# Two transformer blocks on one core: the seams between stages worked token tile by token tile

## The chip, the cores and the metric

The kernel runs on one core of a Trainium2 chip. The time is device microseconds (us) of one execution. Five engines work side by side, each through its own queue in order: PE (TensorE: LDWEIGHTS puts a stationary operand into the array, MATMUL streams a moving operand past it), DVE (VectorE), ACT (ScalarE), POOL (GpSimd), SP (SyncE), which here issues the DMAs. They meet through semaphores.

## What is computed

256 tokens of width 1024, float32. A first block (adaptive norm, three token mixers, output product, norm, a 16-expert mixture with top 2 of one group) ends in a norm; two layers of a second kind follow, and a final norm. The seams that this document is about lie between these steps:

```python
h = x                                        # the first block's output
for l in range(2):
    sh1, sc1, ga1, sh2, sc2, ga2, sh3, sc3, ga3 = split(silu(c) @ ada_w[l] + ada_b[l], 9)
    n = rms_norm(h, norm_g[l, 0]) * (1 + sc1) + sh1
    h = h + 0.5 * ga1 * swiglu(n, ffn_w_in[l, 0], ffn_w_out[l, 0])      # hidden width 2816
    n = rms_norm(h, norm_g[l, 1]) * (1 + sc2) + sh2
    h = h + ga2 * token_mixing(n, mix_w_in[l], ..., mix_w_out[l])       # q, k, v and gates first, mix_w_out last
    n = rms_norm(h, norm_g[l, 2]) * (1 + sc3) + sh3
    h = h + 0.5 * ga3 * swiglu(n, ffn_w_in[l, 1], ffn_w_out[l, 1])
return rms_norm(h, final_norm_g)
# swiglu: gate, up = split(n @ w_in); (silu(gate) * up) @ w_out.  rms_norm: x * rsqrt(mean(x*x) + eps) * g
```

A norm needs the whole row of a token, so it can't begin for a token before that token's last product is summed. It needs nothing of other tokens.

## The kernel before

**Weights.** All weights come as *units* of 128 x 2048 floats (1 MB) in one stream. SP loads a unit into one of three raw slots (`load`, L235 to L241). ACT rounds it to the first float32r half (`conv_hi`, L270) and DVE makes the rest, raw minus that (`conv_lo`, L276). The halves, too, have three slots (`RING = 3`), so `conv_hi` of unit c waits until PE has used unit c-3. Every product is done three times (`mm3`, L343 to L345: high x high, and the two mixed ones) to keep float32 accuracy.

**Which operand is stationary.** In `project` (q, k, v and gates of the mixer; 48 matmuls a unit) the normed tokens are stationary, 128 at a time, and 256 weight columns move; it works tile by tile already. In `rows_product` (down and output products; 24 matmuls a unit) 128 tokens are stationary and 512 weight columns move. In `pe_gate_up` (gate and up products of a feed-forward; 48 matmuls a unit) a 128 x 128 block of the *weights* is stationary, and all 256 tokens move: 2 blocks of columns x 8 depths x 3 products. The hidden layer comes out turned that way, ready for the down product.

**A feed-forward** has 11 groups of 256 hidden columns: gate unit, up unit, and the down unit of the group before. `hidden_order` lays the stream out in that order. ACT takes the silu, DVE multiplies, both split the result. DVE also makes the modulation vectors of later layers from `ada` weights (`half_step`, L304 and L310; two 1 MB loads each from the same SP queue), PE sums them (L324), DVE adds the bias (L338), and PE waits for that before it uses the bank again. `last_down` does the last unit one tile after the other.

**The seam.** After the last product of a stage, all in this order: DVE multiplies tile 0's sum by the gate row and adds it to x (`residual`, L493, L496), then tile 1's. ACT squares tile 0 (L386), POOL makes the root (L395, L397), ACT scales tile 0 (L390) and squares tile 1, POOL makes its root, DVE scales it (L402). PE turns both tiles (`norm_pe`, L418, 8 transposes each) into four banks that hold both tiles side by side, ACT and DVE scale, shift and split them (`spread_act`, `spread_dve`), PE broadcasts the gate (`gate_pe`, L482, 16 matmuls) and ACT copies it out. Then the next stage's first unit begins. There are six such seams (first block's output product to the router; feed-forward to mixer and output product to feed-forward in each layer; feed-forward to feed-forward between the layers), one behind the mixture of experts with two norms in a row, and the final norm.

**Order and loops.** Each engine's order is written out by hand. Groups of a feed-forward, and the 12 q, k and v units, run in hardware loops (`Fori`).

Of the kernel before, what the change touches and what calls it, by code (L numbers as in the profile page):

```python
# [26 lines left out]
P = 128  # L27
# [60 lines left out]
EARLY_HALVES = 20  # L88
FFN_HALVES = {(0, 0): (20, 10), (0, 1): (30, 10), (1, 0): (40, 8), (1, 1): (48, 0)}
# [32 lines left out]
def bass_network(nc, W, AD, x_in, ctx_in, s1_in, s2_in, k1_in, masks_in, gf_in, out):  # L122
    with ExitStack() as ctx:
# [50 lines left out]
        ntmp = z(0, 1024).rearrange("p (b n) -> p b n", b=2)  # L174
# [108 lines left out]
        def load_half(sp, v, e=0):  # L283

            for i in range(2):
                if v > PE_HALVES:
                    sp.wait_ge(ada_used, e * 4 + (2 * (v - 1 - PE_HALVES) + i + 1))
                elif v > 0:
                    sp.wait_ge(ada_used_pe, 2 * (v - 1) + i + 1)
                src = AD[2 * v + i] if isinstance(e, int) and e == 0 else AD[bass.ds(e * 4 + (2 * v + i), 1)].rearrange(  # L290
                    "o p n -> p (o n)")
                sp.dma_start(ada[:, i], src).then_inc(ada_landed[i], 16)

        def half_step(dve, v, n, e=0):

            vv, i, k = v - PE_HALVES, n // 4, n % 4
            cond = 0 if v < B1_HALVES else 16
            if k == 0:
                dve.wait_ge(ada_landed[i], e * 32 + 16 * (v + 1))
            w, c, a = ada[:, i, 512 * k:512 * k + 512], cs[:, cond + n:cond + n + 1], acc[:, v % 2]  # L300
            if n == 0:
                if vv >= 2:
                    dve.wait_ge(ada_sum.sem, e * 2 + (vv - 1))
                ins = nc.vector.tensor_scalar(a, w, c, None, ALU.mult)  # L304
            else:
                if n == 4:
                    dve.wait_ge(ada_used, e * 4 + (2 * vv + 1))
                else:
                    dve.wait_ge(acc_step, e * 12 + (6 * vv + (n if n < 4 else n - 1)))
# [3 lines left out]
        def half_steps(dve, v, i, e=0):  # L313
            for n in range(4 * i, 4 * i + 4):
                half_step(dve, v, n, e)

        def half_sum(pe, v, bank, e=0):

            vv = v - PE_HALVES
            pe.wait_ge(ada_used, e * 4 + (2 * vv + 2))  # L320
            if vv >= 2:
                pe.wait_ge(ada_out.sem, e * 2 + (vv - 1))
# [5 lines left out]
        def half_out(dve, v, bank, e=0):  # L328

            dve.wait_ge(ada_sum.sem, e * 2 + (v - PE_HALVES + 1))  # L330
            b0 = S1["bada"].start
            if isinstance(e, int) and e == 0:
                dst = mod1[:, 4 * v:4 * v + 4] if v < B1_HALVES else mod2[:, 4 * (v - B1_HALVES):4 * (v - B1_HALVES) + 4]
                bias = s1[:, b0 + 4 * v:b0 + 4 * v + 4]
            else:
                dst = mod2[:, bass.ds(e * 8 + 4 * (v - B1_HALVES), 4)]
                bias = s1[:, bass.ds(e * 8 + (b0 + 4 * v), 4)]
            nc.vector.tensor_tensor(dst, PS[:, bank, 0:4], bias, ALU.add).then_inc(*ada_out.up)  # L338
# [8 lines left out]
        def project(u, xh, xl, bank, tiles=range(NT), lo_at=None):  # L347

            wh, wl = (w.rearrange("p (k n) -> p k n", k=DC) for w in u)
            for t in tiles:  # L350
                for k in range(DC):
                    if lo_at and t == 0 and k % 2 == 0:
                        nc.tensor.wait_ge(*lo_at[k // 2])
# [14 lines left out]
        NB = (0, 1, 4, 5)  # L368

        class Norm:  # L370
            def __init__(self, name, per, stats_only=False):
# [4 lines left out]
                self.xa, self.xd, self.am, self.full = (sig(f"{name}_{n}", per) for n in ("scaled0", "scaled1", "factors", "full"))  # L376
# [4 lines left out]
        def norm_act(act, N, k, l, src, dst, x_at=(None, None)):  # L381

            for t in range(NT):
                if x_at[t]:
                    act.wait_ge(*x_at[t])
                nc.scalar.activation(dst[:, t], src[:, t], ACT.Square, scale=D ** -0.5,  # L386
                                     accum_out=st[:, t:t + 1]).then_inc(*N.ss.up)
                if t == 0:
                    act.wait_ge(*N.rstd.at(2 * k, l))
                    nc.scalar.activation(dst[:, 0], src[:, 0], ACT.Copy, scale=st[:, 4:5]).then_inc(*N.xa.up)  # L390
# [8 lines left out]

        def norm_dve(dve, N, k, l, src, dst):  # L400
            dve.wait_ge(*N.rstd.at(2 * k + 1, l))
            nc.vector.tensor_scalar(dst[:, 1], src[:, 1], st[:, 5:6], None, ALU.mult).then_inc(*N.xd.up)  # L402
# [10 lines left out]
        def norm_pe(pe, N, k, l, src, banks):  # L413
            for t, scaled in enumerate((N.xa, N.xd)):
                pe.wait_ge(*scaled.at(k, l))
                for c in range(DC):
                    o = (c % 2) * 256 + t * P
                    ins = nc.tensor.transpose(PS[:, banks[c // 2], o:o + P], src[:, t, c * P:(c + 1) * P], ident)  # L418
                    if t and c % 2:
                        ins.then_inc(*N.turned.up)  # L420

        def spread_act(act, N, k, l, hi, shift, banks, am_):

            act.wait_ge(*N.am.at(k, l))
            for b in range(4):
                act.wait_ge(*N.turned.at(4 * k + b, l))
                for c in range(2):
                    ins = nc.scalar.activation(hi[:, 2 * b + c], PS[:, banks[b], c * 256:(c + 1) * 256], ACT.Identity,
                                               scale=am_[:, 2 * b + c:2 * b + c + 1], bias=shift[:, 2 * b + c:2 * b + c + 1])
                ins.then_inc(*N.hi.up)  # L430
            act.wait_ge(*N.lo.at(4 * k + 1, l))
            for c in range(2):
                ins = nc.scalar.activation(ntmp[:, 1, c * 256:(c + 1) * 256], PS[:, banks[3], c * 256:(c + 1) * 256],
                                           ACT.Identity, scale=am_[:, 6 + c:7 + c], bias=shift[:, 6 + c:7 + c])
            ins.then_inc(*N.full.up)
# [4 lines left out]
        def spread_dve(dve, N, k, l, hi, lo, shift, banks, am_):  # L440
            dve.drain()
            for b in range(4):
                dve.wait_ge(*N.hi.at(4 * k + b, l))
                if b < 3:
                    for c in range(2):
                        nc.vector.tensor_scalar(ntmp[:, b % 2, c * 256:(c + 1) * 256], PS[:, banks[b], c * 256:(c + 1) * 256],
                                                am_[:, 2 * b + c:2 * b + c + 1], shift[:, 2 * b + c:2 * b + c + 1],
                                                ALU.mult, ALU.add)
                    dve.drain()
                else:  # L450
                    dve.wait_ge(*N.full.at(k, l))
# [45 lines left out]

        def at_gate(c0, g):
            return c0 + (3 * g - 1 if g else 0)
# [1808 lines left out]
```

## Time and profile before

| | us |
|---|---|
| median of 3 runs | 2260.92 (2258.34 to 2265.45) |
| profiled execution, its own time | 2261.06 |
| its span, first to last instruction | 2259.3 |
| PE busy | 2008.0 |
| DVE busy | 1388.1 |
| ACT busy | 998.5 |
| mean granted PE clock | 0.924 of 2.4 GHz |

Times of rows count from the span's start. "Busy" of PE is the union of its instructions' durations, which overlap when matmuls follow one another; how far apart they start is read from start times, or from how many (x) lie in a window. PEclk 1.00 is 2.4 GHz, 0.50 is 1.2 GHz.

### The profile page before, as it was taken

The numbers are of one execution on the slowest core, as the hardware profiler recorded it, in microseconds if no ns is written. First come the engines' busy times: TensorE is split into PE (matmuls) and PEld (weight loads), VectorE is DVE, ScalarE is ACT, GpSimd is POOL, SyncE is SP. The second block draws the span as 40 slices with busy tenths as digits, with TensorE's granted clock in tenths as the row PEclk, the third lists the DMA queues.
The fourth block names the chain that finished last, engine by engine and source line by source line (L and its number), as shares of the span: only waits on it lengthen the run. The fifth ranks groups of instructions, "written<-read, shape, count | busy, mean of one in ns | idle before, by whom it ended". The sixth has DMA issues, their size and how long they took to land.

```text
span 2259.3 us, 31283 instructions
## 1 busy us (share of the span) xinstructions
PE 2008.0 (89%) x12630; PEld 1769.3 (78%) x12630; DVE 1388.1 (61%) x1440; ACT 998.5 (44%) x1149; POOL 91.7 (4%) x103
## 2 busy tenths in 40 slices
PE   6878977999999699988797799989998979968997
PEld 1855667888888699978776689978997967857997
DVE  0875755899998677754433677766765343355445
ACT  2423324777777433344345343343334433444333
POOL 0230010000000100010000000000001000000000
PEclk9876786999999899989898899999999989989999
DMA  7563452899998287634312457755763532223553
GB/s 271 199 231 111 164 207 76 324 370 358 348 352 337 114 322 297 254 124 174 106 63 75 149 220 282 283 218 208 299 238 131 176 109 108 75 77 133 191 183 150
DMA packets 63845, 457.93 MB, mean 203 GB/s; under 512 B 7040, under 2 KB 7296, under 8 KB 8832
## 3 DMA queue, kind: packets, MB, share of 16 engines
q1 hardware_dynamic: 63744, 456.51, 53.4%
q8 instruction: 72, 1.18, 0.2%
q14 instruction: 29, 0.24, 0.0%
HBM read 455.43 MB, written 1.05 MB: 202 GB/s over the span
## 4 chain that ended last, share of the span: by engine, by line
issue 40%; PE 39%; DVE 10%; ACT 5%; DMA 3%; POOL 1%; DVEq 1%; POOLq 1%; SPq 0%; ACTq 0%
PE PS L343 10%; PE PS L344 10%; PE PS L345 10%; DVE wlo L276 3%; ACT whi L270 3%; DVE acc L310 2%; DMA ada<-in_ada 2%; PE PS L1158 1%; PE PS L324 1%; DMA raw<-in_stream 1%; PE PS L1701 1%; PE PS L1109 1%; PE PS L1174 1%; POOLq L396 1%; POOL st L397 1%
## 5 line engine op out<-in xcount | busy, mean ns | idle before, releaser
L276 DVE TENSOR_TENSOR wlo<-raw,whi 128x2048 fp32r<-128x2048 f32 x285 | 653.7, 2295 | 514.3 <-ACT whi L270 514.3
L270 ACT ACTIVATE whi<-raw 128x2048 fp32r<-128x2048 f32 x285 | 545.0, 1913 | 496.9 <-PE PS L345 461.1
L343 PE MATMUL PS<-whi,hhi 128*128 128x256 f32 (+1 forms) x1360 | 450.6, 331 | 18.1 <-DVE hlo L466 8.6
L344 PE MATMUL PS<-wlo,hhi 128*128 128x256 f32 (+1 forms) x1360 | 441.4, 325 | 0.0
L345 PE MATMUL PS<-whi,hlo 128*128 128x256 f32 (+1 forms) x1360 | 441.3, 324 | 0.0
L343 PE MATMUL PS<-hhi,whi 128*128 128x256 f32 x1408 | 402.2, 286 | 10.3 <-DVE mod L338 7.7
L344 PE MATMUL PS<-hlo,whi 128*128 128x256 f32 x1408 | 400.2, 284 | 0.0
L345 PE MATMUL PS<-hhi,wlo 128*128 128x256 f32 x1408 | 400.1, 284 | 0.0
L343 PEld LDWEIGHTS PS<-whi,hhi 128*128 128x128 f32 x1360 | 266.5, 196 | 41.1 <-DVE hlo L466 10.1
L343 PEld LDWEIGHTS PS<-hhi,whi 128*128 128x128 f32 x1408 | 272.0, 193 | 14.2 <-DVE wlo L276 8.9
L345 PEld LDWEIGHTS PS<-whi,hlo 128*128 128x128 f32 x1360 | 265.6, 195 | 19.2
L344 PEld LDWEIGHTS PS<-wlo,hhi 128*128 128x128 f32 x1360 | 266.5, 196 | 17.7
L344 PEld LDWEIGHTS PS<-hlo,whi 128*128 128x128 f32 x1408 | 272.1, 193 | 1.4
L345 PEld LDWEIGHTS PS<-hhi,wlo 128*128 128x128 f32 x1408 | 272.0, 193 | 0.0
L343 PE MATMUL PS<-whi,zr 128*128 128x512 f32 (+2 forms) x624 | 233.0, 376 | 21.0 <-DVE zr L1936 11.1
L310 DVE SCALAR_TENSOR_TENSOR acc<-ada,cs,acc 128x512 f32<-128x512 f32 x308 | 238.6, 775 | 10.8 <-DMA ada<-in_ada 1.4
L345 PE MATMUL PS<-whi,zr 128*128 128x512 f32 (+2 forms) x624 | 228.4, 369 | 0.0
L344 PE MATMUL PS<-wlo,zr 128*128 128x512 f32 (+2 forms) x624 | 228.2, 369 | 0.0
L343 PEld LDWEIGHTS PS<-whi,zr 128*128 128x128 f32 (+1 forms) x624 | 114.8, 184 | 41.7 <-DVE zr L1936 11.2
L345 PEld LDWEIGHTS PS<-whi,zr 128*128 128x128 f32 (+1 forms) x624 | 114.7, 184 | 20.8
L344 PEld LDWEIGHTS PS<-wlo,zr 128*128 128x128 f32 (+1 forms) x624 | 114.9, 184 | 18.8
L276 DVE TENSOR_TENSOR wlo<-ada,whi 128x2048 fp32r<-128x2048 f32 x48 | 109.9, 2292 | 12.7 <-ACT whi L270 12.5
(349 smaller groups left out, 1895.5 us busy)
## 6 DMA issues: line engine op xcount, KB each, us to landing
raw<-in_stream SPq DMA_DIRECT2D x285, 1024.0 KB, 4.8
ada<-in_ada SPq DMA_DIRECT2D x96, 1024.0 KB, 4.8
ada<-in_stream SPq DMA_DIRECT2D x48, 1024.0 KB, 4.9
xs<-in_x SPq DMA_DIRECT2D x1, 1024.0 KB, 7.7
Z<-in_ctx SPq DMA_DIRECT2D x1, 1024.0 KB, 9.8
masks<-in_masks SPq DMA_DIRECT2D x2, 512.0 KB, 6.8
Z<-in_gfinal SPq DMA_DIRECT2D x2, 512.0 KB, 7.4
y_out<-Z SPq DMA_DIRECT2D x2, 512.0 KB, 2.6
```

The source lines that it names most:

```text
L270: nc.scalar.activation(whi[:, s], src, ACT.Copy).then_inc(hi_ready, 1)
L276: nc.vector.tensor_tensor(wlo[:, s], src, whi[:, s].bitcast(F32), ALU.subtract).then_inc(lo_ready, 1)
L310: ins = nc.vector.scalar_tensor_tensor(a, w, c, a, ALU.mult, ALU.add)
L324: ins = nc.tensor.matmul(PS[:, bank, c:c + 1], acc[:, v % 2, c * P:(c + 1) * P], ones[:, 0:1], start=True, stop=True)
L343: nc.tensor.matmul(out_, ah, bh, start=start, stop=False, skip_group_check=check)
L344: nc.tensor.matmul(out_, ah, bl, start=False, stop=False, skip_group_check=check)
L345: return nc.tensor.matmul(out_, al, bh, start=False, stop=stop, skip_group_check=check)
L396: pool.drain()
L397: nc.gpsimd.tensor_tensor(st[:, 4 + t:5 + t], st[:, 2 + t:3 + t], k1[:, K1["half"]][:, 0:1], ALU.pow).then_inc(*N.rstd.up)
L1109: ins = nc.tensor.matmul(PS[0:2, 6 + v % 2, :], cs[:, n:16:8], ada[:, i, 512 * k:512 * k + 512], start=n == 0, stop=n == 7)
L1158: nc.tensor.matmul(PS[:, i % 2], q, k, start=i >= 16, stop=True).then_inc(*s_mm.up)
L1174: ins = nc.tensor.matmul(PS[:, 4 + (p // 8) % 2, 64 * (p % 8):64 * (p % 8) + 64], pt[:, p % 2, c * P:(c + 1) * P], v[c], start=c == 0, sto ...
```

## The change

`pe_gate_up` becomes `gate_up_part` with a tile, and the head of a feed-forward does gate 0, up 0 and gate 1 for tile 0, then for tile 1:

```diff
+        def gate_up_part(pe, g, j, c0, E0, tile=None, lo_at=None):
+            wh, wl = (w.rearrange("p (k n) -> p k n", k=DC) for w in unit(pe, at_gate(c0, g) + j, E0))
+            tok = slice(0, S) if tile is None else slice(tile * P, tile * P + P)
+            for f in range(2):
+                for k in range(DC):
+                    w = slice(f * P, (f + 1) * P)
+                    if lo_at and f == 0 and k % 4 == 0:
+                        pe.wait_ge(*lo_at[2 * tile + k // 4])
+                    ins = mm3(PS[:, 2 * (g % 2) + f, j * 256 + tok.start:j * 256 + tok.stop], wh[:, k, w], wl[:, k, w],
+                              hhi[:, k, tok], hlo[:, k, tok], k == 0, k == DC - 1)
+            if tile != 0:
+                ins.then_inc(unit_used, 1)
...
+            head = ((0, 0), (0, 1), (1, 0))
+            for i, (g, j) in enumerate(head):
+                gate_up_part(pe, g, j, c0, E0, 0, None if i else lo_at(k, l))
+                if i == 1:
+                    norm_pe(pe, N2, k, l, 1, xn, TB)
+            for i, (g, j) in enumerate(head):
+                gate_up_part(pe, g, j, c0, E0, 1, None if i else lo_at(k, l))
+            gate_pe(pe, N2, k, l, 6)
```

The down units of the last three groups move to the end of the stream and are done for tile 0, then for tile 1, with the next stage's first transposes between the second and the third:

```diff
+        def last_downs(pe, c0, E0, h0, between):
             for t in range(NT):
+                for g in range(TAIL, FFN_GROUPS):
+                    pe.wait_ge(hlo_done, h0 + (g + 1))
+                    u = unit(pe, at_down(c0, g), E0)
+                    for kk in range(2):
+                        ins = rows_product(u, kk, hid_hi[:, hid(g), kk], hid_lo[:, hid(g), kk], 4, False, False, True, (t,))
+                    if t:
+                        ins.then_inc(unit_used, 1)
+                    if t and g == FFN_GROUPS - 2:
+                        between()
                 for b in range(4 + 2 * t, 6 + 2 * t):
```

`out_product` does its first unit for both tiles, the other three by tile, with `between` in the same place. The mixer does its first three units for tile 0 (tile 1's transposes before the third), then for tile 1. The seam's other engines:

```diff
+        def norm_act(act, N, k, l, shift, c, e, x_at):
+            square_act(act, N, k, l, 0, xs, xn, x_at[0])
+            conv_hi(act, c, e)
+            spread_act(act, N, k, l, 0, hhi, shift, TB, am)
+            conv_hi(act, c + 1, e)
+            conv_hi(act, c + 2, e)
+            square_act(act, N, k, l, 1, xs, xn, x_at[1])
+            scale_act(act, N, k, l, xs, xn)
+            spread_act(act, N, k, l, 1, hhi, shift, TB, am)
+
+        def norm_dve(dve, N, k, l, shift, c, e, y_at):
+            residual(dve, N.x_new, 0, y_at[0])
+            scale_dve(dve, N, k, l, xs, xn)
+            conv_lo(dve, c, e)
+            spread_dve(dve, N, k, l, 0, hhi, hlo, shift, TB, am)
+            residual(dve, N.x_new, 1, y_at[1])
+            conv_lo(dve, c + 1, e)
+            dve.wait_ge(*N.rstd.at(2 * k + 1, l))
+            conv_lo(dve, c + 2, e)
+            spread_dve(dve, N, k, l, 1, hhi, hlo, shift, TB, am)
```

`scale_dve` scales tile 0 and `scale_act` tile 1, the other way round than before. `spread_act` and `spread_dve` now work on one tile: ACT writes the first four blocks of 128 columns into a buffer, DVE the other four, ACT copies each half out rounded, DVE subtracts. The gate's diagonal on POOL waits for tile 1's last split (`N2.lo`), its broadcast on PE comes after the three first units. In the last two groups of a feed-forward, which have no down product beside them, the conversions stand behind silu and behind the rounding:

```diff
+                if g <= TAIL:
+                    conv_hi(act, c + RING, E0)
+                act_silu(act, g, c0, E0, h0)
+                if g > TAIL:
+                    conv_hi(act, at_gate(c0, g) + RING, E0)
+                else:
+                    conv_hi(act, c + 1 + RING, E0)
+                act_hi(act, g, c0, E0, h0)
```

Behind the mixture of experts, two conversions that stood ahead of the norm stand behind its two tiles' steps. The conversions behind the last feed-forward are gone. All `Fori` loops are written out.

## Rows read from the trace of the kernel before

**Rows 1.** of the page: busy time, and the chain that ended last, by engine.
```profile
PE 2008.0 (89%) x12630; PEld 1769.3 (78%) x12630; DVE 1388.1 (61%) x1440; ACT 998.5 (44%) x1149; POOL 91.7 (4%) x103
...
issue 40%; PE 39%; DVE 10%; ACT 5%; DMA 3%; POOL 1%; DVEq 1%; POOLq 1%; SPq 0%; ACTq 0%
```

**Rows 2.** waits of PE, whole span: us in total, times, longest us.
```profile
PE PS L418 <- ACT xn L390: 51.3, 7, 13.4
...
PE PS L343 <- DVE mod L338: 7.7, 3, 3.2
```

**Rows 3.** windows around five stage boundaries: us, busy (xcount) by engine, PEclk, DMA, GB/s.
```profile
745.40:787.00 41.60, 25.09 (x181) 23.95 (x181) 28.44 (x31) 16.77 (x25) 10.56 (x9) 0.79 0.20 76
957.00:1002.50 45.50, 36.94 (x229) 33.50 (x230) 26.52 (x25) 19.81 (x24) 7.81 (x10) 0.85 0.31 111
1267.10:1322.40 55.30, 47.16 (x276) 41.98 (x277) 30.36 (x31) 22.70 (x25) 4.40 (x5) 0.91 0.38 144
1494.20:1541.20 47.00, 37.20 (x235) 33.21 (x235) 30.50 (x33) 19.89 (x24) 5.22 (x5) 0.89 0.39 153
1713.00:1759.20 46.20, 36.52 (x231) 32.46 (x230) 27.13 (x24) 20.46 (x25) 7.27 (x10) 0.89 0.31 113
```

**Rows 4.** windows of PE alone: us, PE busy (xcount), PEclk, DMA share, GB/s.
```profile
1317.00:1328.00 11.00, 11.00 (x94) 1.00 0.46 167
1275.00:1285.00 10.00, 10.00 (x46) 1.00 0.43 133
1102.00:1104.00 2.00, 2.00 (x37) 1.00 0.03 8
351.00:354.00 3.00, 3.00 (x16) 0.50 0.06 11
395.00:741.00 346.00, 346.00 (x1630) 1.00 0.90 349
1131.00:1165.00 34.00, 32.42 (x226) 0.98 0.18 63
183.00:245.00 62.00, 57.23 (x188) 0.50 0.32 117
```

**Rows 5.** timeline of PE, matmuls with 256 columns after a boundary.
```profile
984.99 0.41 PE L344 MATMUL PS<-wlo,hhi 128*128 128x256 f32 x1
985.20 0.41 PE L345 MATMUL PS<-whi,hlo 128*128 128x256 f32 x1
```

**Rows 6.** window of the same stretch, all engines, for its PEclk.
```profile
984.70:985.50 0.80, 0.80 (x6) 0.80 (x5) 0.80 (x3) 0.59 (x2) 0.00 (x0) 0.50 0.00 0
```

**Rows 7.** timeline, group 9 of the first feed-forward: start us, us, engine, line, count.
```profile
938.14 0.98 PEld L324 LDWEIGHTS PS<-k,acc 128*128 128x128 f32 x8
938.26 0.95 PE L324 MATMUL PS<-k,acc 128*128 128x1 f32 x8
...
938.95 1.91 ACT L270 ACTIVATE whi<-raw 128x2048 fp32r<-128x2048 f32 x1
...
940.89 2.29 DVE L276 TENSOR_TENSOR wlo<-raw,whi 128x2048 fp32r<-128x2048 f32 x1 [0.54 <-ACT whi L270]
```

**Rows 8.** timeline at the boundary after the first output product: the norm chain.
```profile
1288.31 1.22 DVE L493 TENSOR_TENSOR Z<-PS,row 128x1024 f32<-128x1024 f32 x1
...
1291.50 1.06 ACT L386 ACTIVATE xn<-xs 128x1024 f32<-128x1024 f32 x1 [5.76 <-DVE xs L496]
...
1292.72 1.23 POOL L395 TENSOR_TENSOR st<-st,k 128x1 f32<-128x1 f32 x1 [2.34 <-ACT xn L386]
...
1295.86 1.97 PE L418 MATMUL PS<-k,xn 128*128 128x128 f32 x8 [6.70 <-ACT xn L390]
...
1297.84 0.75 DVE L402 TENSOR_SCALAR xn<-xs,st 128x1024 f32<-128x1024 f32 x1 [3.94 <-POOL st L397]
...
1299.43 3.76 ACT L428 ACTIVATE hhi<-PS,mod,am 128x256 fp32r<-128x256 f32 x8 [0.78 <-PE PS L418]
...
1301.56 0.69 DVE L452 TENSOR_TENSOR hlo<-Z,hhi 128x512 fp32r<-128x512 f32 x1
```

More of the change, by code:

```diff
@@ L326, in half_sum, with half_out @@
             ins.then_inc(*ada_sum.up)
[L328 to L338, printed above, removed]
+        def half_out(dve, v, bank):
+            dve.wait_ge(*ada_sum.at(v - PE_HALVES))
+            b0 = S1["bada"].start + 4 * v
+            dst = mod1[:, 4 * v:4 * v + 4] if v < B1_HALVES else mod2[:, 4 * (v - B1_HALVES):4 * (v - B1_HALVES) + 4]
+            nc.vector.tensor_tensor(dst, PS[:, bank, 0:4], s1[:, b0:b0 + 4], ALU.add).then_inc(*ada_out.up)
         def mm3(out_, ah, al, bh, bl, start, stop, check=False):
@@ L375, in __init__ @@
                     return
-                self.xa, self.xd, self.am, self.full = (sig(f"{name}_{n}", per) for n in ("scaled0", "scaled1", "factors", "full"))
+                self.scaled = [sig(f"{name}_scaled{t}", per) for t in range(NT)]
+                self.fullB = sig(f"{name}_full", 2 * per)
+                self.am = sig(f"{name}_factors", per)
                 self.turned, self.hi, self.lo = (sig(f"{name}_{n}", 4 * per) for n in ("turned", "hi", "lo"))
@@ L411, in turn @@
                     ins.then_inc(*done.up)
[L413 to L422, printed above, removed]
-            act.wait_ge(*N.am.at(k, l))
[L425 to L435, printed above, removed]
@@ L487, in gate_act @@
             nc.scalar.activation(row[:, :], PS[:, bank:bank + 2].rearrange("p b n -> p (b n)"), ACT.Copy).then_inc(*N.row.up)
-        def residual(dve, done, y_at, banks=((4, 5), (6, 7)), tmp=ytmp):
-            for t in range(NT):
-                dve.wait_ge(*y_at[t])
-                nc.vector.tensor_tensor(tmp[:, t], PS[:, banks[t][0]:banks[t][1] + 1].rearrange("p b n -> p (b n)"), row[:, :],
-                                        ALU.mult)
-                dve.drain()
-                nc.vector.tensor_tensor(xs[:, t], xs[:, t], tmp[:, t], ALU.add).then_inc(*done.up)
@@ new lines, in hidden_pe @@
+        def hidden_pe(pe, c0, E0, h0, halves, k, l, between):
+            v0, nh = halves
+            head = ((0, 0), (0, 1), (1, 0))
[6 more added lines that the diff above has]
+            gate_pe(pe, N2, k, l, 6)
+            for g in range(1, FFN_GROUPS):
+                steps, sums = g < nh, g <= nh
+                if sums and g > 1:
+                    pe.wait_ge(*ada_out.at(v0 + g - 2 - PE_HALVES))
+                elif nh and g > 1:
+                    pe.wait_ge(*ada_out.at(v0 + nh - 1 - PE_HALVES))
+                for j in range(int(g == 1), 2):
+                    gate_up_part(pe, g, j, c0, E0)
+                if sums:
+                    pe.wait_ge(h_made, h0 + g)
+                    half_sum(pe, v0 + g - 1, 2 * (1 - g % 2))
+                if g == 1:
+                    pe.wait_ge(*N2.row.at(k, l))
+                    clear_sums(pe)
+                if g <= TAIL:
+                    pe_down(pe, g - 1, c0, E0, h0)
+            last_downs(pe, c0, E0, h0, between)
@@ L2121, in _ @@
                 hidden_sp(sp, FF0, E0, FFN_HALVES[l, 0])
-                with sp.Fori(0, MIX_UNITS // RING) as e:
-                    for j in range(RING):
-                        load(sp, QK0 + RING + j, E0 + e)
+                for j in range(MIX_UNITS):
+                    load(sp, QK0 + RING + j, E0)
                 hidden_sp(sp, FF1, E0, FFN_HALVES[l, 1])
@@ L2219, in hidden_order @@
     seq = [gate[0], up[0]]
-    for g in range(1, n):
+    for g in range(1, n - 2):
         seq += [gate[g], up[g], down[g - 1]]
-    return seq + [down[n - 1]]
+    for g in range(n - 2, n):
+        seq += [gate[g], up[g]]
+    return seq + down[n - 3:]
 def halves(w):
```

522 lines of the change are left out of this document (260 added, 262 removed).

## The prediction

> **What bounds the kernel now.** I began with the page. PE is busy for 2008 of 2259 us and holds the largest named share of the chain that ended last [rows 1], so time goes if PE work goes, or PE's waits. The waits view names the largest wait: transposes for the scaled tile, 51.3 us in 7 pieces, the longest 13.4 [rows 2]. Those are the seams. The window view then prices a seam with all around it: what PE does, and at what clock [rows 3]. In the five windows PE's clock averages 0.79 to 0.91; the reader is to see that a seam costs twice, in waiting and in matmuls at 1.2 GHz behind it. Between seams PE has no gap: 346 us of 346 in the mixture of experts [rows 4]. Last I read how far apart matmuls of each shape start, since the change makes new shapes.
>
> **The distance of matmuls.** In a window with x of them it is its length over x, less the two or three under way at its start. At full clock: 256 moving columns 0.120 us (94 in 11 us), 512 columns 0.227 (46 in 10), 128 columns past a stationary of only 32 columns 0.060 (37 in 2) [rows 4]. At half clock, 20 moving columns past a stationary of 128: 16 in 3 us, 0.213 [rows 4]; and 256 moving columns: 985.20 - 984.99, also 0.21 [rows 5], at clock 0.50 [rows 6]. So with a full stationary operand 20 columns cost as much as 256: the loading sets the distance. At full clock, eight loads with one moving column take 0.98 us [rows 7], 0.12 each with the last one's run-out in it, so a little less from start to start; and half of 0.213, the clock being twice as fast, is 0.107. Hence a load of 128 columns costs about 0.112, hidden behind 256 moving columns but not behind 128.
>
> This is where the change pays. In `project`, `rows_product` and the output product the tokens are stationary, so doing a unit by tile adds nothing: the same matmuls in another order. In a feed-forward's head the weights are stationary: 3 units x 48 = 144 matmuls of 256 columns become 288 of 128, each with its load. At 0.112 they take 32.3 us in place of 144 x 0.120 = 17.3: +15.0 us in each of four feed-forwards, 60 in all. The bounds: not below the 0.060 of the small stationary (17.3 us, adds nothing), not above the 0.120 of 256 columns (34.6 us, +17.3, 69 in all). I take 0.112, as only the 0.060 row has another stationary, and it is the smaller load that makes it fast.
>
> The Trainium skill (TensorE: Matmul & The Clock Gate, LDWEIGHTS (loading the stationary operand)) gives a load as its columns over 1.2 GHz, 107 ns for 128: the trace agrees within 6 ns. The same page, in Back-to-back issue gap, gives a stream of load and matmul pairs at 128 columns about 81 ns each; by that the term would be some 6 us each and 24 in all. No row here shows a full load under 0.11. I keep it as a rival.
>
> **Seam by seam.** PE work first, then waits. Work common to all: 16 transposes and 16 gate matmuls at 0.112, 2.0 (with their turnaround) and 1.8.
>
> *The norm chain of a tile.* Before: multiply begins 1288.31, ACT's square 1291.50, POOL 1292.72, transposes 1295.86 [rows 8]. That is 7.5 us. Now DVE scales tile 0 (0.75, where ACT's stands for 1.1), and POOL's diagonal no longer runs beside the add, which I put at 0.6: some 6.6. Beside it PE has tile 1 of two units, 24 x 0.227 = 5.4. So the transposes come 1.25 late. From them to the first split block I reckon four small scalings (under ACT's 3.76 / 8 = 0.47 each), a copy of about 0.6 and a subtraction of 0.69 [rows 8], 3.3; PE has the third unit's tile 1, 2.7: late by 0.2 to 0.6.
>
> *Feed-forward to mixer, twice.* Work: three down units 72 x 0.227 = 16.3, closing sums 0.9, 2.0, three units 17.3, gate 1.8: 38.3. Waits: the second down unit can only be converted behind the last silu. Silu done 0.8 after the last up unit, ACT 1.9, DVE 2.3 [rows 7]: 5.0, against 2.7 of the first down unit's tile 0. That wait is new, 2.3 us (1.3 in layer 0, where the L324 sums of 0.95 lie in it), and 0.2 for the third. Transposes 1.25, split 0.2. The mixer's second unit then waits for DVE, which must finish the split of tile 0, tile 1's residual (2.5) and the conversion (2.3): 2.55 late. Sum of waits 5.5 and 6.5, so 43.9 and 44.8. Before, the same span without one down unit (5.45) was 45.5 and 46.2 [rows 3], so 51.0 and 51.6: -7.1 and -6.8.
>
> *Output product to feed-forward, twice.* Work: 96 x 0.227 = 21.8, 2.0, 32.3, 1.8, clearing 0.9: 58.8. Waits 1.25 and 0.6. Here the longer tile-0 part (16 us) covers all of tile 1's chain. 60.6 against 55.3 [rows 3]; the second layer's seam repeats it: +5.3 each.
>
> *Feed-forward to feed-forward.* 16.3 + 0.9 + 2.0 + 32.3 + 1.8 + 0.9 = 54.2, waits 1.3, 0.2, 1.25, 0.6: 57.6. Before 47.0 [rows 3] + 5.45 = 52.4: +5.2.
>
> *Behind the mixture of experts.* Nothing of the old stage is left to lie beside the norms. Two conversions leave the way of the final norm (4.6 of DVE), but one still stands between the tiles; I reckon the first matmul 4 us earlier, at 18.4 of the window. Then 288 x 0.112, 2.4 for a start at half clock, 1.0 + 1.8 + 0.9: 56.8 against 41.6 [rows 3]: +15.2.
>
> *The rest.* Start of the first block, seam to the router (all 256 tokens are needed, so only a part overlaps) and the final norm: each has something earlier and something later (the last gains the two conversions on DVE and pays the 2.3 us wait). Together +0.6, bounds -6 and +8 by one chain of rows 8 gained or lost.
>
> *A wait that goes.* PE waits 7.7 us in three pieces for the modulation's bias (L338) early in three feed-forwards [rows 2]: after a seam SP's queue holds the next unit's load behind two `ada` loads that wait for DVE. The longer head gives that queue time for what it has to bring. I take it as gone, and with it the half clock behind the two longer ones, which I put at 4.5 us (an estimate: windows with such waits stand at 0.84 to 0.89 in rows 3): -12.2. Bounds: 0 and -12.2.
>
> *Half clock at the new seams.* The waits left are shorter than the old ones, but come one behind the other. Every old seam had some half clock [rows 3]. For the two mixer seams I take 1.7 each, 3.4; bounds 0 and 8.
>
> *Written-out loops.* Instructions come from memory as before. 346 us of written-out code show PE without a gap [rows 4]: 0. [...]
>
> **Sum**, on the span of 2259.3: 15.2 + 5.3 + 5.3 + 5.2 - 7.1 - 6.8 + 0.6 - 12.2 + 3.4 = +8.9, so 2268.2; with the 1.8 between span and time 2270.0. The profiled execution (2261.06) is within 0.2 of the median (2260.92), so the same number stands for the median.
>
> **Rivals.**
> *A. Loads hidden behind 128 columns* (each pair 0.060 to 0.081). For: at 0.060 the array can take a pair that fast [rows 4]. Against: rows 4, 5 and 7, three cases with a full load. At 0.060 the head is 15.0 us shorter in each feed-forward, but tile 1's chain is then only covered by half: some 4 of it come back each time. 2270 - 60 + 16 = 2226. This is the faster case. By the skill's 81 ns it would be 2270 - 36 = 2234.
> *B. The heads run at half clock.* In 62 us of attention PE was busy for 57 and the clock stayed at 0.50; with 20 columns per load it stayed there too [rows 4]. At 128 columns per load the array streams half of the time. For it: those rows. Against it: 34 us of small matmuls in the mixer at 0.98 [rows 4]. It decides when the clock doesn't rise again behind a seam: each head takes up to 288 x (0.213 - 0.112) = 29 us more. In one to four of the heads: 2299 to 2386.
> *C. The chains are wholly covered* and nothing of my waits appears: 5.5 + 6.5 + 1.9 x 2 + 3.4 + 3.4 = 22 less, 2248. For: they rest on orders of queues that I worked out. Against: the silu's place ahead of the conversion is in the code.
> *D. The wait for the bias stays*: 2282.
>
> **Chances.** Forecast 0.58 (2270, own range 2256 to 2282), A 0.10, B 0.14, C 0.10, D 0.08. A measurement of this kernel tells 0.3%, 6.8 us, from no change. Faster by more: A, C and a little of the forecast: 0.20. Slower by more: B, D and about two thirds of the forecast: 0.60. Within: 0.20. The range leaves out A and half of B: 2246 to 2305.
>
> **What would show it.** In the changed trace, gate and up matmuls of 128 columns: their distance at full clock, 0.112 (right) or near 0.06 (A), and PEclk over the heads (B). A gap of 2.3 us ahead of the second-to-last down unit's tile 0, and one of 2.5 ahead of the mixer's second unit. Waits for the scaled tile down from 51 to some 15. No wait for L338 early in a feed-forward. The forecast fails if PE's busy time doesn't grow by some 50 us.

## The result and the profile after

| | before | after |
|---|---|---|
| median, us | 2259.63 (4 runs, 2256.13 to 2265.45) | 2287.93 (4 runs, 2284.42 to 2288.71) |
| profiled execution, its own time | 2261.06 | 2284.42 |
| its span | 2259.3 | 2282.7 |
| PE busy | 2008.0 | 2062.2 |
| mean granted PE clock | 0.924 | 0.932 |

Ratio 1.0113, 95% interval 1.009 to 1.0136: slower. 2270 was forecast, with a range of 2246 to 2305. The sign and the main term were right; the sum was +8.9 where the spans differ by 23.4 us (the medians by 28.3). The result lies in the wide range, which had room for the rivals, but outside the forecast's own 2256 to 2282.

Busy time of the changed kernel, the page's row (its answer to the first row of [rows 1]):

```profile
PE 2062.2 (90%) x13206; PEld 1823.3 (80%) x13206; DVE 1369.9 (60%) x1455; ACT 996.3 (44%) x1164; POOL 83.2 (4%) x103
```

PE has 576 more matmuls (4 heads x 144) and is 54 us busier, while DVE has 18 us less. The waits view of PE (engine, line, releaser: us in all, times, longest) answers to [rows 2]:

```profile
PE PS L427 <- DVE xn L404: 13.2, 1, 13.2
...
PE PS L351 <- DVE mod L346: 12.4, 5, 4.7
PE PS L351 <- DVE wlo L277: 11.3, 6, 2.2
```

L427 is the old L418, L351 the old L343, L346 the old L338, L277 the old L276. Of the 51.3 us for the scaled tile, 13.2 are left in this row, and 7.9 more for ACT's half at the router. The wait for the bias has grown from 7.7 to 12.4, with a longest of 4.7, where I had struck it out. The six waits for the weights' conversion are the ones that I forecast: four at the ends of the feed-forwards, two at the mixer's second unit.

The five boundaries again, same columns as [rows 3], each from the matching instruction. Three of the five hold one down unit (5.45 us) that the old windows don't: the second, fourth and fifth.

```profile
741.50:805.30 63.80, 48.07 (x319) 47.70 (x320) 26.45 (x33) 19.41 (x27) 9.21 (x9) 0.70 0.14 50
977.10:1020.30 43.20, 39.42 (x255) 34.38 (x254) 28.05 (x29) 24.68 (x30) 6.72 (x10) 1.00 0.38 131
1282.90:1341.70 58.80, 58.00 (x417) 53.55 (x417) 30.19 (x34) 22.24 (x26) 3.86 (x5) 1.00 0.36 134
1512.70:1568.10 55.40, 53.82 (x398) 49.04 (x398) 33.70 (x38) 23.15 (x27) 3.85 (x5) 1.00 0.41 153
1730.30:1777.10 46.80, 42.08 (x253) 36.91 (x252) 27.91 (x28) 25.15 (x30) 6.72 (x10) 0.93 0.35 123
```

In the last four PE now has 0.8 to 4.7 us of gaps where it had 8 to 10, at clock 0.93 to 1.00 where it had 0.85 to 0.91: the tiles do cover each other's norm chains. But the third is 3.5 us longer than before all the same, because it is full of loads (288 matmuls of 128 columns in place of 144 of 256). And in the first, behind the mixture of experts, the clock fell from 0.79 to 0.70, and it is 22 us longer.

How far apart the new matmuls start, from windows of PE alone (us, PE busy (xcount), PEclk, DMA share, GB/s), inside the heads:

```profile
1318.00:1328.00 10.00, 10.00 (x93) 1.00 0.15 60
...
785.00:795.00 10.00, 10.00 (x92) 1.00 0.00 0
...
762.00:772.00 10.00, 10.00 (x48) 0.50 0.00 0
```

92 or 93 matmuls of 128 columns in 10 us, less the two or three under way: 0.110 to 0.111 us each. At half clock it is 0.213. So the load of 128 stationary columns sets the distance, and rival A is out. The head behind the mixture of experts ran tile 0's first 96 matmuls, all that stand ahead of tile 1's transposes, at 0.213.

The timeline around 957 us (start, us, engine, line, count; the bracket is the idle time before and its releaser) shows the wait that I had not foreseen:

```profile
957.04 0.95 PE L337 MATMUL PS<-k,acc 128*128 128x1 f32 x8
957.24 0.60 ACT L560 ACTIVATE Z<-PS 128x512 f32<-128x512 f32 x1 [9.54 <-PE PS L353]
957.73 1.90 ACT L271 ACTIVATE whi<-raw 128x2048 fp32r<-128x2048 f32 x1
957.86 0.69 DVE L572 TENSOR_TENSOR Z<-Z,PS 128x512 f32<-128x512 f32 x1 [5.08 <-ACT Z L560]
959.53 0.62 ACT L567 ACTIVATE zr<-Z 128x512 fp32r<-128x512 f32 x1
959.66 2.29 DVE L277 TENSOR_TENSOR wlo<-raw,whi 128x2048 fp32r<-128x2048 f32 x1 [1.11 <-ACT whi L271]
960.05 1.90 ACT L271 ACTIVATE whi<-raw 128x2048 fp32r<-128x2048 f32 x1
961.87 0.68 DVE L576 TENSOR_TENSOR zr<-Z,zr 128x512 fp32r<-128x512 f32 x1
...
962.47 0.15 DVE L346 TENSOR_TENSOR mod<-PS,s 128x4 f32<-128x4 f32 x1
...
962.68 0.58 PE L351 MATMUL PS<-hhi,whi 128*128 128x256 f32 x1 [4.70 <-DVE mod L346]
```

PE sums the modulation (L337) and wants that bank again for its next gate unit. DVE frees it by adding the bias, 0.15 us of work, but does so last: behind a conversion, which itself waits for ACT, and behind the hidden layer's split. Before, a down product of 5.45 us stood between PE's two steps and covered this. The same add in the kernel before, 5.45 us behind PE's sums at 938.26, and PE's next gate unit, which doesn't wait:

```profile
943.71 0.15 DVE L338 TENSOR_TENSOR mod<-PS,s 128x4 f32<-128x4 f32 x1
...
944.64 0.28 PE L343 MATMUL PS<-hhi,whi 128*128 128x256 f32 x1
```

The change took the down products of the last three groups away, and with them the cover. It happens in both feed-forwards of layer 0, at 958 and at 1493 us, 4.70 us each time, and each leaves half clock behind:

```profile
1496.40:1503.20 6.80, 5.22 (x24) 0.50 0.46 154
960.50:967.30 6.80, 4.62 (x21) 0.50 0.47 154
```

### The profile page after: what moved, and what is told of

It is laid out like the page before. It is cut to its first block, busy times and chain, and to the rows that moved or that the text cites. A ratio compares the mean times of both kernels' runs of the same rounds, so it can differ in the third digit from the quotient of the medians.

```text
span 2282.7 us, 30949 instructions
## 1 busy us (share of the span) xinstructions
PE 2062.2 (90%) x13206; PEld 1823.3 (80%) x13206; DVE 1369.9 (60%) x1455; ACT 996.3 (44%) x1164; POOL 83.2 (4%) x103
## 4 chain that ended last, share of the span: by engine, by line
issue 80%; PE 8%; DVE 5%; ACT 2%; DMA 2%; POOL 1%; DVEq 0%; POOLq 0%; ACTq 0%; SPq 0%
DVE acc L324 2%; DMA ada<-in_ada 2%; DVE wlo L277 1%; PE PS L351 1%; PE PS L353 1%; PE PS L352 1%; PE PS L1182 1%; PE PS L1131 1%; ACT whi L271 1%; PE PS L1198 1%; POOL Z L483 1%; DVE hlo L460 1%; PE PS L1189 1%; ACT Z L439 1%; PE PS L337 0%
## 5 line engine op out<-in xcount | busy, mean ns | idle before, releaser
L277 DVE TENSOR_TENSOR wlo<-raw,whi 128x2048 fp32r<-128x2048 f32 x282 | 646.9, 2295 | 467.5 <-ACT whi L271 461.8
L271 ACT ACTIVATE whi<-raw 128x2048 fp32r<-128x2048 f32 x282 | 538.3, 1912 | 410.6 <-PE PS L353 379.8
L351 PE MATMUL PS<-hhi,whi 128*128 128x256 f32 (+1 forms) x1600 | 457.5, 286 | 16.5 <-DVE mod L346 12.4
L351 PE MATMUL PS<-whi,hhi 128*128 128x256 f32 (+1 forms) x1360 | 451.0, 332 | 22.4 <-DVE hlo L473 8.9
L352 PE MATMUL PS<-hlo,whi 128*128 128x256 f32 (+1 forms) x1600 | 456.4, 285 | 0.0
L353 PE MATMUL PS<-hhi,wlo 128*128 128x256 f32 (+1 forms) x1600 | 456.2, 285 | 0.0
L351 PEld LDWEIGHTS PS<-hhi,whi 128*128 128x128 f32 x1600 | 314.0, 196 | 20.7 <-DVE mod L346 13.8
L352 PEld LDWEIGHTS PS<-hlo,whi 128*128 128x128 f32 x1600 | 314.0, 196 | 1.1
L353 PEld LDWEIGHTS PS<-hhi,wlo 128*128 128x128 f32 x1600 | 313.9, 196 | 0.0
L351 PEld LDWEIGHTS PS<-whi,hhi 128*128 128x128 f32 x1360 | 266.8, 196 | 46.3 <-DVE hlo L473 10.4
L351 PE MATMUL PS<-whi,zr 128*128 128x512 f32 (+2 forms) x624 | 234.2, 378 | 28.3 <-DVE zr L1976 11.1
L351 PEld LDWEIGHTS PS<-whi,zr 128*128 128x128 f32 (+1 forms) x624 | 115.2, 185 | 50.3 <-issue 19.7
L560 ACT ACTIVATE Z<-PS 128x512 f32<-128x512 f32 x44 | 26.3, 597 | 209.7 <-PE PS L353 209.7
```

What stands on the lines that cost most here:

```text
L271: nc.scalar.activation(whi[:, s], src, ACT.Copy).then_inc(hi_ready, 1)
L277: nc.vector.tensor_tensor(wlo[:, s], src, whi[:, s].bitcast(F32), ALU.subtract).then_inc(lo_ready, 1)
L351: nc.tensor.matmul(out_, ah, bh, start=start, stop=False, skip_group_check=check)
L352: nc.tensor.matmul(out_, ah, bl, start=False, stop=False, skip_group_check=check)
L353: return nc.tensor.matmul(out_, al, bh, start=False, stop=stop, skip_group_check=check)
L560: nc.scalar.activation(hs, PS[:, p:p + 2, 0:256], ACT.Silu).then_inc(silu_done, 1)
```

## The experiments

Ratios are to the kernel before, timed in the same session, with 95% intervals. The changed kernel itself stands at 1.0113. Of the edits, lines that only select a form, and the wait of a whole head for both tiles' splits, are left out.

**heads_whole.** The heads' matmuls have 256 columns again; everything else is as changed.

```diff
-            for i, (g, j) in enumerate(head):
-                gate_up_part(pe, g, j, c0, E0, 0, None if i else lo_at(k, l))
-                if i == 1:
-                    norm_pe(pe, N2, k, l, 1, xn, TB)
-            for i, (g, j) in enumerate(head):
-                gate_up_part(pe, g, j, c0, E0, 1, None if i else lo_at(k, l))
+            norm_pe(pe, N2, k, l, 1, xn, TB)
+            for i, (g, j) in enumerate(head):
+                gate_up_part(pe, g, j, c0, E0, None, None if i else lo_at(k, l))
```

> The changed kernel with the four feed-forward heads not split: tile 1 is turned first, then gate 0, up 0 and gate 1 run with 256 moving tokens. Everything else of the change stays. Theory (loading 128 columns sets the distance, 0.111 us in the changed trace, 0.213 at half clock): the heads' 288 matmuls become 144 at 0.120, 15 us less of PE work in each of four, and about 10 us more in the head behind the mixture of experts, which ran at half clock; given back is the wait for tile 1's chain, about 11 us in three heads and a few us in the first. From the traces: 4.6 us less in each of three, 18 to 22 less in the first, 32 to 36 us less in all than the changed kernel's 2288: about 2254. Rival (the split itself is free and the loss lies elsewhere, in new waits at the ends of the feed-forwards): PE work is the same and the chain is exposed, so 25 to 35 us slower than the changed kernel, about 2318.

Measured: 0.9954 (0.9939 to 0.997), 2253.5 us. Undoing this one part wins back 1.6% and leaves a kernel faster than the one before, so the split heads are what turned the change's sign. The waits view now shows what they had covered, PE waiting for tile 1 (one of the four, 7.9 us at the router, is in the changed kernel too):

```profile
PE PS L427 <- ACT xn L400: 31.3, 4, 7.9
```

From the start of tile 0's transposes to the gate broadcast, the first head takes 26.5 us in place of 48.9; the three others 35.1, 35.6 and 35.1 in place of 37.6. So without the split each of those wins 2.0 to 2.5 us, not the 4.6 expected, and the first makes up most of the gain (22.3 us).

**head_one_whole.** The same edit at the first head alone, `if (k, l) == (0, 0)`.

> As the changed kernel, but only the head behind the mixture of experts is not split (nothing of an old stage lies beside its norms). Theory (that head pays the loads, 15 us, and on top half clock, since 128 columns to a load don't bring the clock up, some 10 us): 18 to 22 us less than 2288, about 2268, and PEclk rises to 1.00 within a few us of the head's start where it stayed at 0.50 for 24 us. Rival (the clock there is only the time of day after a 13 us wait, whatever runs): the clock stays at 0.50 for the same 24 us, and at 0.213 for 256 columns too the whole head takes 31 us at most, so 5 to 10 us less.

Measured: 0.9985 (0.9974 to 0.9997), 2259.3 us; the profiled span is 26.8 us shorter than the changed kernel's. That is 80% of what all four whole heads bring, and more than the 18 to 22 expected. 22.3 us of it lie in the head. Another 3.0 are half clock at the second mixer seam, which the changed kernel's trace has and this one hasn't, though the edit touches nothing there; the rest is spread over later stages. The same windows of PE as above, now from this kernel: the stretch ahead of the head and its start, then 10 us inside it.

```profile
746.00:766.00 20.00, 7.08 (x32) 0.50 0.31 105
766.50:776.50 10.00, 10.00 (x86) 1.00 0.01 2
```

PE's first gate matmul is at 762.6 here, at half clock, and the full clock is back at 766.5, 4 us later. In the changed kernel it began at 759.2 and the clock stayed at 0.50 until 783.0, 24 us with no gap. Ahead of it stand 16 transposes and a gap of 3.9 us here, 8 transposes and a gap of 2.5 us there, and it starts 3.4 us later; otherwise only the columns per load differ. (86 in 10 us, less those under way, is again 0.120.)

**warm_up.** The changed kernel, with dummy matmuls ahead of the first head, where PE idles:

```diff
+                for i in range(56):
+                    nc.tensor.matmul(PS[:, 4], zb[:, 0:P], zb[:, :], start=True, stop=True)
                 norm_pe(pe, N2, 0, 0, 0, xn, TB)
+                for i in range(11):
+                    nc.tensor.matmul(PS[:, 4], zb[:, 0:P], zb[:, :], start=True, stop=True)
```

> The changed kernel, with 56 dummy matmuls of 512 bf16 columns ahead of the first head's first transposes (PE was idle there) and 11 behind them; nothing else. In the changed kernel the head behind the mixture of experts began at clock 0.50 and its 96 matmuls of tile 0 took 20.7 us, 0.213 each, without a gap. Theory: 128 columns per load don't bring the clock up, but don't let it fall either; begun at full clock, tile 0's part takes 96 x 0.111 = 10.7 us, so 10 to 12 us less than the changed kernel, about 1.005 times the kernel before. Rival: in this stretch the clock is down for another reason (the rest of the chip, or the columns per load alone), and the head falls back to 0.50 however it begins: no gain, about 1.011.

Measured: 1.0046 (1.0032 to 1.0059), 2274.8 us, 0.7% or some 15 us under the changed kernel (10.0 by the spans; 11.4 from tile 0's transposes to the gate broadcast). Windows of PE: the dummies, tile 0's 96 matmuls, tile 1's and the rest of tile 0's 192.

```profile
742.00:754.20 12.20, 12.13 (x54) 0.98 0.20 75
759.50:770.30 10.80, 10.80 (x97) 1.00 0.01 2
771.10:792.60 21.50, 21.50 (x195) 1.00 0.11 38
```

Begun at full clock, the same split head stays there for all of its 33 us, and tile 0's part takes 10.9 us instead of 20.7. The rival (it falls back whatever comes before) is out.

**bias_early.** In the last two groups DVE adds the bias right behind the hidden product:

```diff
                 dve_h(dve, g, h0)
+                if sums and g > TAIL:
+                    half_out(dve, v0 + g - 1, 2 * (1 - g % 2))
...
-                if sums:
+                if sums and g <= TAIL:
                     half_out(dve, v0 + g - 1, 2 * (1 - g % 2))
```

> The changed kernel with one order changed: in the last two groups of a feed-forward DVE adds the modulation bias (L346) right behind the hidden product, ahead of the weight conversion. Theory: PE's two waits of 4.70 us ahead of the last gate unit in the two feed-forwards with modulation work there come from this order, since the down unit that used to cover them has moved to the end; they shrink to about 0.9, and the half clock behind them (2.2 us each) goes: 10 to 12 us less than 2288, about 2277. Rival (they wait for the conversion of the last gate unit's weights as well): same time, the wait now named after L277.

Measured: 1.0044 (1.003 to 1.0057), 2271.4 us; the span is 13.7 us shorter than the changed kernel's. The wait is down from 4.70 to 0.69, and no half clock follows; of this kernel's timeline:

```profile
959.70 0.69 DVE L572 TENSOR_TENSOR Z<-Z,PS 128x512 f32<-128x512 f32 x1 [5.08 <-ACT Z L560]
960.31 0.15 DVE L346 TENSOR_TENSOR mod<-PS,s 128x4 f32<-128x4 f32 x1
960.52 0.39 PE L351 MATMUL PS<-hhi,whi 128*128 128x256 f32 x1 [0.69 <-DVE mod L346]
```

2 x (4.70 - 0.69) is 8.0 us of waiting. From the gate broadcast to the next stage's first transposes the two feed-forwards of layer 0 are 4.2 and 6.4 us shorter, 10.6 in all, with the clock behind the waits. The other 3.0 us are again the half clock at the second mixer seam, where this edit changes no wait. So the trace shows some 11 us for moving one instruction of 0.15 us.

**conv_early.** In the last two groups the conversion of the next unit stands ahead of silu (on ACT) and of the half steps (on DVE), as in the other groups:

```diff
-                if g <= TAIL:
-                    conv_hi(act, c + RING, E0)
+                conv_hi(act, at_gate(c0, g) + RING, E0)
                 act_silu(act, g, c0, E0, h0)
-                if g > TAIL:
-                    conv_hi(act, at_gate(c0, g) + RING, E0)
-                else:
+                if g <= TAIL:
                     conv_hi(act, c + 1 + RING, E0)
...
```

> The changed kernel with the conversion of the last two groups' next unit put back ahead of silu on ACT and ahead of the hidden product on DVE. Theory: the waits of 1.25, 1.25, 2.16 and 2.16 us between the first and second down unit's tile 0 go, with one stretch of half clock behind: 7 to 9 us less than 2288, about 2280. The two 4.70 us waits get a little shorter too, as DVE converts unit 29 before the hidden product instead of behind it: up to 4 more. Rival (the second down unit then waits for its load or its slot instead): no change.

Measured: 1.0066 (1.004 to 1.0091), 2275.5 us. The waits of PE in this kernel, against 12.4 (longest 4.7) and 11.3 in the changed one:

```profile
PE PS L351 <- DVE mod L346: 8.5, 5, 2.7
...
PE PS L351 <- DVE wlo L277: 6.1, 4, 2.2
```

The forecast wait for the second down unit was real, and the conversion's place in the queue made it: it is gone in layer 0 (1.25 us, twice) and down from 2.16 to 0.83, twice, in layer 1. The bias wait shrinks too, since a conversion no longer stands ahead of it.

**loops_written_out.** The kernel before, `with X.Fori(a, b) as e:` replaced by `for e in range(a, b):` in all six places.

> The kernel before with all six of its hardware loops written out, nothing else. My prediction put this part of the change at 0: ratio 0.998 to 1.002. [...] One more row speaks for a small gain: from the first block's seam to the router the changed kernel was 4 us ahead of the kernel before.

Measured: 0.9992 (0.9979 to 1.0004). No effect of this part is seen either way; and the changed kernel's 4 us lead at the router isn't from it.

**heads_whole_early.** heads_whole, bias_early and conv_early together (edits as above).

> The changed kernel with three edits together: the heads of the feed-forwards whole (256 columns), the bias added right behind the hidden product in the last groups, and the conversions of the last groups ahead of silu. Heads whole alone stood at 0.9954, bias early and conversions early took 0.7% and 0.5% off the changed kernel. If these are separate losses, the sum is 0.9954 - 0.006 - 0.002 (the two share the 4.7 us waits): 0.986 to 0.990, about 2235 us. Rival: with the heads whole the waits in the last groups are already covered otherwise: 0.995.

Measured: 0.9894 (0.9872 to 0.9915), 2240.7 us. The losses are separate but for the overlap that was reckoned with; the result is at the upper end of what was expected.

**one_unit_by_tile.** On top of that, the first unit of the three later heads by tile:

```diff
-                norm_pe(pe, N2, k, l, 1, xn, TB)
-                for i, (g, j) in enumerate(head):
-                    gate_up_part(pe, g, j, c0, E0, None, None if i else lo_at(k, l))
+                gate_up_part(pe, 0, 0, c0, E0, 0, lo_at(k, l))
+                norm_pe(pe, N2, k, l, 1, xn, TB)
+                gate_up_part(pe, 0, 0, c0, E0, 1, lo_at(k, l))
+                for i, (g, j) in enumerate(head[1:]):
+                    gate_up_part(pe, g, j, c0, E0)
```

> The same combined kernel, but in the three later heads the first unit (48 matmuls of 256 columns) is done tile by tile, 96 of 128. Cost by my prices: 96 x 0.111 - 48 x 0.120 = 4.9 us a head. Gain: with whole heads PE waits 7.9, 7.5 and 7.9 us for tile 1's transposes, with some 13.6 us at half clock behind; tile 0's part (5.3 us) covers 5.3 of it. Theory: gain and cost cancel, within 0.2% of the combined kernel, with the shorter half clock as a small gain (up to 2 us a head). Rival: doing work by tile with stationary weights never pays: 3 x 4.9 = 15 us, 0.65%, slower.

Measured: 0.9944 (0.9927 to 0.9961), 2250.7 us: 10 us slower than the combined kernel, so I was wrong and the rival nearer. Windows of PE at the head after the first output product: tile 0's 48 matmuls, tile 1's 48, and the first of 256 columns behind them.

```profile
1279.70:1285.20 5.50, 5.50 (x48) 1.00 1.01 427
1290.70:1301.10 10.40, 10.37 (x49) 0.50 0.15 61
1301.10:1305.10 4.00, 4.00 (x20) 0.50 0.00 0
```

Between tile 0's and tile 1's part PE waited 1.7 and 2.7 us, the clock fell, and tile 1's part took twice its time at 0.213 each. Again the clock rose only 4 us after the first matmul of 256 columns.

**whole_kept_warm and one_unit_kept_warm.** Both kernels with dummy matmuls in the waits of the heads. The first:

```diff
+                for i in range(0 if (k, l) == (0, 0) else 34):
+                    nc.tensor.matmul(PS[:, 4], zb[:, 0:P], zb[:, :], start=True, stop=True)
                 norm_pe(pe, N2, k, l, 1, xn, TB)
+                for i in range(15 if (k, l) == (0, 0) else 9):
+                    nc.tensor.matmul(PS[:, 6], zb[:, 0:P], zb[:, :], start=True, stop=True)
```

and 56 ahead of the first head's transposes, as in warm_up.

> The combined kernel (heads whole, bias and conversions early) with dummy matmuls in PE's waits at the four heads: 56 and 15 around the first head's transposes, 34 and 9 around tile 1's transposes at the other three, each 512 bf16 columns into a bank that is free there; they took 0.227 each in the run before. The combined kernel has some 14 us at clock 0.50 at each of the three heads, in which PE does 16 transposes or part of them and some 4 us of matmuls, and 20 at the first. Kept at full clock these save about 2.5 us at each of the three and 3.2 at the first: 10 us, ratio 0.985 against 0.9894. Rival: the dummies themselves delay the head, or the chip takes the clock away later instead: 0.989 to 0.993.

> The kernel with one unit of the three later heads by tile, with dummy matmuls in its waits (7 ahead of tile 1's transposes, 11 behind them; 56 and 15 at the first head). Without them it stood at 0.9944, 10 us above the combined kernel where I had expected none, and in its trace tile 1's 48 matmuls of 128 columns took 10.2 us, at clock 0.50, which lasted 17 us instead of 14. Theory: that half clock is the whole excess, 3 x 5 us; with the clock kept, cost (4.9) and cover (5.3) cancel: 0.984 to 0.987, the same as the combined kernel kept warm. Rival: the split costs more by itself: 5 us or more (0.2%) above that kernel.

Measured: 0.9835 (0.9822 to 0.9848), 2226.7 us, the fastest of all; and 0.985 (0.9834 to 0.9867), 2230.1 us. One window of PE from the second kernel, tile 1's part, for the 10.4 us above:

```profile
1289.30:1294.80 5.50, 5.47 (x49) 1.00 0.27 113
```

With the clock kept, the two kernels are 3.4 us apart instead of 10, and their intervals overlap. From tile 0's transposes to the gate broadcast, this head takes 32.9 us whole and 32.6 with one unit split, and the two later ones the same; without the dummies it was 35.0 and 39.2. So the split cancels out, as reckoned, and its loss was the clock. The fill itself brought 0.6%, 14 us where I expected 10. (A dummy starts 0.216 us behind the one before, not 0.227.) The kernel before was not run with dummies, so how much of the 0.9835 the fill would bring without any work by tile isn't shown.

**heads_by_tile_mended.** The changed kernel with its heads as they were, and warm_up, bias_early and conv_early together.

> The changed kernel with its heads by tile as they were (three units, 128 columns per load), and all else mended: warm start of the first head, bias and conversions early in the last groups. It says what the heads by tile cost at their best, against the whole heads kept warm (0.9835). Theory: 4 x 15 us of loads less the waits for tile 1 that they cover at the three later heads (7.9 + 2.3, 7.5 + 2.3, 7.9 + 2.3 = 30) and some 4 at the first: 60 - 34 = 26 us above 2227, ratio 0.995. From the other side: 1.0046 for the warm start alone, less 0.7 to 0.9% for the two early edits: 0.996 to 0.998. Rival: the parts interfere, and it stays over 1.000.

Measured: 0.9973 (0.9964 to 0.9983), 2256.8 us. That is 30 us over whole_kept_warm, with every other flaw mended in both. From tile 0's transposes to the gate broadcast each head takes 37.5 to 37.6 us, against 24.9 for the first and 32.9 to 33.0 for the others: 26.5 us in the four heads, where 26 was expected. This is the price of the split heads: 60 us of loads against some 34 us of covered waits.

## Why the prediction was right in sign and short in size

**Distance of matmuls: right.** 0.112 was taken, 0.110 to 0.111 measured; 54 us more PE busy time where some 50 were asked for. Rival A fell with it. The half-clock row did the work: a doubled clock halves 0.213. The Trainium skill (TensorE: Matmul & The Clock Gate, LDWEIGHTS (loading the stationary operand)) gives 107 ns for such a load; at full clock the trace agrees, with starts 110 to 111 ns apart. The same page of the Trainium skill, in Back-to-back issue gap, gives 81 ns a pair at 128 columns; no window here shows that, and the measured 110 to 111 ns stand.

**The seams with full clock: right in direction, each within 2.5 us.** From down unit or output product to the same landmark behind it, measured against forecast: -7.8 and -4.8 (forecast -7.1 and -6.8, with 1.7 each of half clock to come on top), +3.5 and +3.5 (+5.3 each), +3.0 (+5.2). One term made most of the difference: the norm chain of a tile was reckoned at 6.6 us and took 5.5, because POOL's add takes 0.19 us here and 1.23 in [rows 8]. The 0.6 that I took off was for DVE's addition, which takes 1.86 us beside POOL's diagonal (five times in the kernel before) and 1.23 alone; this second collision I left in. In the kernel before, each of the six POOL adds of 1.2 us began during DVE's addition for tile 1 and ended within 0.1 us of it, as the one of [rows 8] at 1292.72 did:

```profile
1292.67 1.23 DVE L496 TENSOR_TENSOR xs<-xs,Z 128x1024 f32<-128x1024 f32 x1
```

In the changed kernel that addition comes later. So the transposes, forecast 1.25 late, never were. Half clock came at the second mixer seam alone, and cost 3.0 us there. The waits for the second down unit (1.25 and 2.16 us, forecast 1.3 and 2.3) and the mixer's second unit (2.23 and 2.24, forecast 2.55) were where I put them. Of the chain after, at the first mixer seam, DVE's multiplication, POOL's add and the transposes:

```profile
987.74 1.23 DVE L499 TENSOR_TENSOR Z<-PS,row 128x1024 f32<-128x1024 f32 x1 [3.25 <-PE PS L552]
...
991.53 0.19 POOL L409 TENSOR_TENSOR st<-st,k 128x1 f32<-128x1 f32 x1 [205.11 <-ACT xn L395]
...
993.24 0.99 PE L427 MATMUL PS<-k,xn 128*128 128x128 f32 x7
```

**Behind the mixture of experts: wrong by 7 us.** Forecast +15.2, measured +22.2. The failed term is the 2.4 us "for a start at half clock": it supposed that a full stream of matmuls brings the clock back, which 128 columns per load didn't do for 24 us. Tile 0's first 96 matmuls alone took 9.8 us more than in warm_up. This was rival B's mechanism, to which I gave 0.14, and it struck at one head of four, the only one that began at half clock. The other three began at full clock and kept it.

**A wait that goes: wrong by 20 us, the largest miss.** The step said that PE's waits for L338 go, with 4.5 us of clock, -12.2. In the three feed-forward bodies that it spoke of, the changed kernel was 7.8 us slower (+7.3 and +4.7 in layer 0, -4.2 in layer 1). The early waits did shrink, to 1.7, 0.66 and 0.63. But two new ones of 4.70, with half clock behind, took their place. Nor was the longer head what shrank the early ones: with whole heads they are 0.28, 1.79 and 0.26. (The 4.5 us of clock stood on windows of [rows 3], which hold none of these waits; behind the two longer ones, at 1337 and 1557 us, 3.4 and 5.7 us ran at half clock, which is some 4.6 us lost, so that figure was right by luck.) I had asked what stands behind the moved conversions only for PE's wait on those conversions. I had not asked who waits for the other instructions that they now delay, nor what the removed down product had covered. Shown by bias_early. Of the 7.8, the waits and their clock account for about 5; some 3 us there stay unexplained.

**The rest: forecast +0.6, measured -4.0**, inside the bounds of -6 and +8. Nearly all of it is a lead of 4.1 us at the router's first product, of which 2.9 us were won in the seam ahead of it; no run took it apart.

**Loops written out: right**, 0 forecast, a ratio of 0.9992 measured.

By these pieces: 8.9 + 7 + 20, less 12.6 for the seams and the rest that came out cheaper, is 23.3; the spans differ by 23.4. That 12.6 us of errors went the other way is luck: the two misses alone would have made it some 36. Rival C's covered chains thus came true in part (the transposes), and so did rival D's staying wait, in another place than it named. Two omissions of one sign made a forecast of "barely slower" into a plain loss.

## What to carry to other kernels

Splitting a stage by token tile adds no PE work where the tokens are the stationary operand and costs a whole set of loads where the weights are: here 4.9 us per unit, for 5.3 us of work to hide a wait behind. So it can win next to nothing (0.4 us a head in the kernels kept warm). When a unit of work leaves a stretch, list every wait that lay beside it, the 0.15 us instructions too, and where each stands in its queue. Where PE must wait, dummy matmuls that end with the wait can be worth more than the wait looks: 0.6% here.

## What the hardware did that I had not expected

The clock granted to a stream of matmuls depended on the clock at which the stream began. Three windows of PE, the first two from the changed kernel and the third from one_unit_by_tile above:

```profile
759.20:783.00 23.80, 23.80 (x112) 0.50 0.00 1
...
1307.00:1340.00 33.00, 33.00 (x297) 1.00 0.46 177
...
1290.70:1301.10 10.40, 10.37 (x49) 0.50 0.15 61
```

Streams of matmuls, each with its load, without a gap:

| began at | columns per load | what the clock did |
|---|---|---|
| 0.50 (changed kernel, 759 us) | 128 | 0.50 for 24 us, then 1.00 |
| 0.50 (one unit by tile, 1290.7) | 128 | 0.50 for all 10.4 us |
| 0.50 (first head whole, 762.6) | 256 | 1.00 after 4 us |
| 1.00 (warm start, 759.5) | 128 | stayed 1.00 for 33 us |
| 1.00 (changed kernel, 1307, 1533, 2065) | 128 | stayed 1.00 |

At half clock a load of 128 columns takes 0.213 us, so the penalty on such a stream is the full factor of two. In the first row the clock rose at 783.0, in the midst of matmuls of 128 columns and 3.3 us after tile 1's eight transposes began, so such a stream can run into a rise. What makes the clock rise, these runs don't show. The first row is a single stretch; the second happened at all three later heads of that kernel (39.0 to 39.3 us each, from tile 0's transposes to the gate broadcast). Other stretches of 256 columns were back at full clock after up to 5.7 us (in the kernel before, 1556.7 to 1562.4).
